# Column sums moved into the last product tile, and a new order of work at the joints

## What is computed

```
def rms_norm(x, w):
    x32 = x.astype(jnp.float32)
    y = x32 * lax.rsqrt(jnp.mean(x32 * x32, axis=-1, keepdims=True) + EPS)
    return (y * w.astype(jnp.float32)).astype(x.dtype)
...
        h = rms_norm(x, mix_norm_pre[l]) * (1.0 + sc_m[:, None, :]) + sh_m[:, None, :]
        y = hybrid_mixer(h, positions, w_in[l], ...)
        x = x + g_m[:, None, :] * rms_norm(y, mix_norm_post[l])
        h = rms_norm(x, ffn_norm_pre[l]) * (1.0 + sc_f[:, None, :]) + sh_f[:, None, :]
        y = swiglu(h, w_gate_up[l], w_down[l])
        x = x + g_f[:, None, :] * rms_norm(y, ffn_norm_post[l])
```

## Time and profile before

| | us |
|---|---|
| median of 3 runs | 3138.99 |
| lowest, highest run | 3138.62, 3145.86 |
| span of the profiled execution | 3139.0 |
| TensorE busy in it | 3038.9 (97%) |
| VectorE busy | 1677.1 (53%) |
| GpSimd busy | 1394.7 (44%) |
| ScalarE busy | 1235.8 (39%) |

### The profile page before, as it was taken

How to read it: one execution, slowest core, us unless ns; L and a number is a source line. 1 busy time by engine, 2 the same in 40 slices (tenths; PEclk the granted TensorE clock), 3 DMA queues, 4 the chain that set the end, 5 groups by cost and what they waited for, 6 DMA issues and landing times.

```text
span 3139.0 us, 40030 instructions
## 1 busy us (share of the span) xinstructions
PE 3038.9 (97%) x14910; PEld 2422.7 (77%) x14910; DVE 1677.1 (53%) x2917; ACT 1235.8 (39%) x2444; POOL 1394.7 (44%) x1196
## 2 busy tenths in 40 slices
PE   6999899999999999999999999999999999999998
PEld 5677778888776788888867687888887677888886
DVE  7787656623677553223385746554245656565521
ACT  3345432233345432233354534434334545343432
POOL 2331255545432254445542545444464335454443
PEclk9998899998999899999999999999999999999999
DMA  5422346632421122322331122232232211223222
GB/s 219 126 86 100 122 169 245 243 105 77 125 81 41 41 84 95 100 93 89 119 101 41 54 81 81 94 101 96 96 110 90 81 48 61 94 81 101 94 93 75
DMA packets 92977, 316.54 MB, mean 101 GB/s; under 512 B 12016, under 2 KB 12656, under 8 KB 92656
## 3 DMA queue, kind: packets, MB, share of 16 engines
q1 hardware_dynamic: 92784, 313.99, 30.1%
HBM read 301.36 MB, written 2.10 MB: 97 GB/s over the span
## 4 chain that ended last, share of the span: by engine, by line
PE 91%; DVE 5%; ACT 1%; issue 1%; DMA 1%; POOL 0%; SPq 0%; DVEq 0%; ACTq 0%
PE bank L199 24%; PE bank L200 23%; PE bank L201 23%; PE bank L1831 2%; PE bank L1852 2%; PE bank L1885 2%; PE bank L418 1%; PE bank L419 1%; DVE sel L1351 1%; PE bank L422 1%; PE bank L534 1%; PE bank L1118 1%; PE bank L958 1%; DVE small L1350 1%; PE bank L432 1%
## 5 line engine op out<-in xcount | busy, mean ns | idle before, releaser
L182 POOL TENSOR_TENSOR wl<-raw,wh 128x512 fp32r<-128x512 f32 (+1 forms) x952 | 1241.0, 1308 | 1571.8 <-ACT wh L171 1571.1
L171 ACT ACTIVATE wh<-raw 128x512 fp32r<-128x512 f32 (+1 forms) x952 | 587.7, 623 | 1369.9 <-PE bank L201 1273.2
L199 PE MATMUL bank<-hh,wh 128*128 128x512 f32 x2368 | 945.6, 399 | 0.8 <-DVE hl L1516 0.4
L200 PE MATMUL bank<-hl,wh 128*128 128x512 f32 x2368 | 925.2, 391 | 0.0
L201 PE MATMUL bank<-hh,wl 128*128 128x512 f32 x2368 | 924.9, 391 | 0.0
L199 PEld LDWEIGHTS bank<-hh,wh 128*128 128x128 f32 x2368 | 446.0, 188 | 128.7 <-issue 34.6
L201 PEld LDWEIGHTS bank<-hh,wl 128*128 128x128 f32 x2368 | 446.0, 188 | 95.5
L200 PEld LDWEIGHTS bank<-hl,wh 128*128 128x128 f32 x2368 | 446.3, 188 | 89.2 <-issue 0.5
L201 PE MATMUL bank<-hidh,wl 128*128 128x512 f32 x704 | 273.9, 389 | 0.0
L199 PE MATMUL bank<-hidh,wh 128*128 128x512 f32 x704 | 273.9, 389 | 0.0
L200 PE MATMUL bank<-hidl,wh 128*128 128x512 f32 x704 | 273.9, 389 | 0.0
(11 more groups left out here) (395 smaller groups left out, 4159.9 us busy)
## 6 DMA issues: line engine op xcount, KB each, us to landing
raw<-in_w SPq DMA_DIRECT2D x444, 512.0 KB, 3.4
mod_raw2a<-in_wmod SPq DMA_DIRECT2D x28, 512.0 KB, 4.6
mod_raw2b<-in_wmod SPq DMA_DIRECT2D x28, 512.0 KB, 4.8
mod_raw<-in_wmod SPq DMA_DIRECT2D x24, 512.0 KB, 4.2
raw<-in_w SPq DMA_DIRECT2D x32, 384.0 KB, 3.0
first_mods<-in_wmod SPq DMA_DIRECT2D x16, 512.0 KB, 13.8
tmp<-rawb SPq DMA_DIRECT2D x72, 64.0 KB, 2.4
turn<-sine SPq DMA_DIRECT2D x56, 64.0 KB, 2.0
```

Source lines behind the costliest of these rows:

```text
L171: act.activation(self.m.wh[:, t % 2, w_], self.m.raw[:, t % RING, w_], ACT.Copy)\
L182: pool.tensor_tensor(self.m.wl[:, t % 2, w_], self.m.raw[:, t % RING, w_], self.m.wh[:, t % 2, w_].bitcast(F32), ALU.subtract)\
L199: pe.matmul(out, wh, xh, start=start, stop=False)
L200: pe.matmul(out, wh, xl, start=False, stop=False)
```

## The change

The sums over acc, gain_sum and cross_sum (24 passes) leave the junction; TensorE does them in the last weight tile of the product, ahead of its last chunk (`first_columns`). In the last junction it is the 8 passes over acc. The sums over the last cross product go ahead of the first spread instead of behind it. That cross product is now made by VectorE from the bank, with the gain, without waiting for y (L401 of the new file), and ScalarE makes y's last tile behind the first root (`last_output`). VectorE does the mean ahead of its first multiply, the second reciprocal right behind it, then adds tile 0, multiplies tiles 1, 2 and 4 by acc (no longer by bank 5), and tile 5 between the first scales. GpSimd waits for the copied inverse alone and multiplies tiles 3, 6 and 7. Two scales and two rests now alternate.

```
+        def first_columns(pe):
+            pe.wait_ge(cross_used if carry else square_used, KD - 1)
+            for tb in range(NT):
+                column(pe, ps[4][:, 2 * tb:2 * tb + 1], m.acc, tb, ones[:, 0:1], start=(tb == 0))
+            if carry:
+                for tb in range(NT):
+                    column(pe, ps[4][:, 2 * tb + 1:2 * tb + 2], gain_sum, tb, ones[:, 0:1])
+                for tb in range(NT):
+                    column(pe, ps[1][:, tb:tb + 1], cross_sum, tb, ones[:, 0:1], start=(tb == 0))
...
                     if c == 3:
                         last.then_inc(s.slot_done[0], 1)
+                    if t == n - 1 and c == s.width(t) // P - 2:
+                        first_columns(pe)
...
+        def last_output(act):
+            act.wait_ge(cross_ready, KD)
+            act.activation(m.y[:, KD - 1, :], ps[banks[(KD - 1) % 2]][:], ACT.Identity, scale=gain[:, KD - 1:KD])\
+               .then_inc(y_ready, 1)
...
+                if carry and last:
+                    dve.wait_ge(square_ready, KD)
+                    dve.scalar_tensor_tensor(m.sq[:, 0, :], ps[banks[nb % 2]][:], gain[:, nb:nb + 1], m.x[:, nb, :],
+                                             ALU.mult, ALU.mult).then_inc(cross_ready, 1)
...
-        OWN = 5
+        OWN = [0, 1, 2, 4, 5]
+        SHARED = [3, 6, 7]
...
-            pool.wait_ge(x_ready, 1)
             pool.wait_ge(inv_copied, 1)
-            pool.wait_ge(col_ready, 2)
+            multiply(3)
+            pool.wait_ge(x_ready, 1)
             update(1)
             update(2)
-            multiply(5)
             update(3)
             multiply(6)
             update(4)
             update(5)
+            update(6)
             multiply(7)
-            update(6)
             update(7)
...
             if pre:
+                last_output(act)
+                act.wait_ge(mean_ready, 1)
+                act.activation(xroot4, mean4, ACT.Sqrt, bias=m.eps[:, 0:1], scale=1.0 / D).then_inc(root_ready, 1)
                 act.wait_ge(added_ready, 1)
                 act.activation(m.acc[:], ps[5][:], ACT.Copy).then_inc(inv_copied, 1)
-                act.wait_ge(mean_ready, 1)
...
-                dve.tensor_tensor(m.y[:, k, :], m.y[:, k, :], ps[5][:], ALU.mult).then_inc(added_ready, 1)
+                inv = m.acc if k else ps[5]
+                dve.tensor_tensor(m.y[:, k, :], m.y[:, k, :], inv[:], ALU.mult).then_inc(added_ready, 1)
```

More of the change, by code:

```diff
@@ L286, in swap_halves, with column @@
             sp.dma_start(dst[at + 32:at + 64], src[at:at + 32]).then_inc(sem, 16)
+    def column(pe, dst, src, tb, w, start=False, stop=False):
+        return pe.matmul(dst, src[:, tb * P:(tb + 1) * P], w, start=start, stop=stop)
     OUT_SEMS = ("square_ready", "square_used", "y_ready", "cross_ready", "cross_used", "weights_set")
@@ L360, in scalar @@
                         act.activation(square(nb), ps[banks[nb % 2]][:], ACT.Square).then_inc(square_ready, 1)
-                    act.activation(m.y[:, nb, :], ps[banks[nb % 2]][:], ACT.Identity, scale=gain[:, nb:nb + 1])\
-                       .then_inc(y_ready, 1)
+                    if nb < KD - 1 or not carry:
+                        act.activation(m.y[:, nb, :], ps[banks[nb % 2]][:], ACT.Identity, scale=gain[:, nb:nb + 1])\
+                           .then_inc(y_ready, 1)
                     if nb < KD - 1:
@@ L381, in vector @@
                         dve.wait_ge(cross_used, nb)
-                    dst = m.sq[:, 0, :] if last else ps[0][:]
-                    dve.tensor_tensor(dst, m.x[:, nb, :], m.y[:, nb, :], ALU.mult).then_inc(cross_ready, 1)
+                    dve.tensor_tensor(ps[0][:], m.x[:, nb, :], m.y[:, nb, :], ALU.mult).then_inc(cross_ready, 1)
                 if last:
@@ L405, in vector @@
                     ins.then_inc(cross_used, 1)
-        return Stage(sync, gpsimd, tensor, scalar, vector)
+        stage = Stage(sync, gpsimd, tensor, scalar, vector)
+        stage.last_output = last_output
+        return stage
     START_SEMS = ("square_ready", "square_used", "xroot_ready", "xdiag_ready", "xinv_ready", "scaled_ready",
@@ L489, in build, with junction @@
               "scaled_ready", "h_head_ready", "h_ready", "order")
[L491 removed]
+    def junction(sems, product, pre, last_output, cols=None):
         (sum_ready, root_ready, col_ready, inv_ready, inv_copied, mean_ready, added_ready, multiplied, x_ready,
@@ L544, in tensor @@
             for tb in range(NT):
-                ins = column(ps[4][:, 2 * tb:2 * tb + (2 if pre else 1)], m.sq[:, 1, :], tb, w_, stop=(tb == NT - 1))
+                ins = column(pe, ps[4][:, 2 * tb:2 * tb + (2 if pre else 1)], m.sq[:, 1, :], tb, w_, stop=(tb == NT - 1))
             ins.then_inc(sum_ready, 1)
             if pre:
+                pe.wait_ge(cross_ready, KD)
                 for tb in range(NT):
-                    column(ps[1][:, tb:tb + 1], cross_sum, tb, ones[:, 0:1], start=(tb == 0))
+                    ins = column(pe, ps[1][:, tb:tb + 1], m.sq[:, 0, :], tb, ones[:, 0:1], stop=(tb == NT - 1))
+                ins.then_inc(sum_ready, 1)
             pe.wait_ge(col_ready, 1)
@@ L552, in tensor @@
             if pre:
[L553 to L556, removed]
                 pe.wait_ge(col_ready, 2)
@@ L617, in vector @@
             dve.tensor_scalar(mean4, mean4, 0.0, None, ALU.max).then_inc(mean_ready, 1)
+            dve.wait_ge(inv_ready, 1)
+            add(0)
+            dve.wait_ge(root_ready, 2)
+            dve.reciprocal(xinv4, xroot4).then_inc(col_ready, 1)
+            dve.wait_ge(added_ready, 1)
+            dve.tensor_tensor(m.x[:, 0, :], m.x[:, 0, :], m.y[:, 0, :], ALU.add).then_inc(x_ready, 1)
             dve.wait_ge(inv_copied, 1)
             add(1)
[L620 to L623, removed]
+            add(2)
+            add(4)
             dve.wait_ge(inv_ready, 2)
@@ L626, in vector @@
             scale(1)
[L627 to L630, removed]
+            rest(0)
+            add(5)
+            scale(2)
+            rest(1)
+            rest(2)
+            scale(3)
+            scale(4)
+            rest(3)
+            rest(4)
+            scale(5)
+            scale(6)
+            rest(5)
+            rest(6)
+            scale(7)
+            rest(7)
         stage = Stage(None, gpsimd if pre else None, tensor, scalar, vector)
```

25 lines of the change are left out of this document (10 added, 15 removed).

## The result

The changed kernel takes 3172.3 us (median of 6 runs, 3166.2 to 3175.6), the kernel before 3138.8 (6 runs, 3132.6 to 3154.5). The ratio is 1.010, 95 % interval 1.0076 to 1.0124: it is slower. The profiled execution has a span of 3164.5 us; it is the shortest of the six (3166.2 us). Of all runs in this document one stands apart, in a slower state: one of fold_fill's nine took 4582 us at a granted clock of 0.61, and its ratio leaves it out.

The account below looks back on a forecast made before the run. TensorE, busy 3038.9 of 3139.0 us, plus its waits bounds the kernel. Per joint 8.8 + 7.1 + 13.3 = 29.2 against 24.86, +4.3 for seven joints, plus 0.85 at the end: 31 us, giving 3170 us, range 3150 to 3180.

Parts of the forecast that it names:

- part 1: Last tile: 24 moved sum passes get no cover, so the product ends 2.6 us later, losing 0.85 us of cover.
- rival (d): Last tile: moved passes slide between product matmuls at no cost; 2.3 us a joint faster, 3123 us; chance 6 %.
- part 2: Joint, from mark (old start of first sum pass) to VectorE's first multiply: 8.8 us against mean 5.26, loss 3.5.
- Rival (b): Joint's sums: clock holds through them, first multiply after 7.3 us, 10 us less in all, 3160 us; chance 10 %.
- part 3: Joint, second spread: reciprocal right behind first multiply, second inverse there after 2.95 us instead of 4.94; 2.0 us won.
- rival (a): Multiplies before first scale: turns cost less, first multiply to matmul 4.9 us, 2.2 less a joint, 3155 us; chance 12 %.
- part 4: First multiply to next stage: VectorE's multiplies take turns with GpSimd over SBUF; 7.1 us against mean 6.45, loss 0.65.
- part 5: Next stage's first matmul to first ordinary one: TensorE stays the bound by 0.9 us; 13.3 us against mean 13.1.
- The last joint: Very end of the kernel: 8 moved passes, formerly covered by the square, cost 0.85 us.
- Spare time of cross_used: Wait of first_columns for cross_used: costs nothing, with 0.1 us to spare in the out product.

Follow-up runs that it names:

- fold_fill: Changed kernel with sums behind the product, bank-5 multiplies, last cross product added into cross_sum by VectorE, and throwaway matmuls in TensorE's waits; 3129.6 us, ratio 0.9972.
- only_cols: Kernel before, with only the sums over acc, gain sum and cross sum moved ahead of the last chunk; 3163.5 us, ratio 1.0081.
- bank_reads: Changed kernel, with VectorE's multiplies reading the inverse from bank 5 again instead of acc; 3154.4 us, ratio 1.0044.
- pool_held: Changed kernel, still reading acc, with GpSimd's first multiply held until VectorE has done its first four; one run, 3163.8 us.
- fill_before: Kernel before, with throwaway 512-column matmuls in each of seven joints, three ahead of the second spread and three behind it; 3140.6 us, ratio 1.0000.
- cols_back: Changed kernel, with the sum passes behind the product's last chunk again; 3154.2 us, ratio 1.005.
- fill_both: Changed kernel with sums behind the last chunk, bank-5 multiplies, and throwaway matmuls, two ahead of the second spread and three behind; 3138.0 us, ratio 0.9996.
- both_back: Changed kernel with sums behind the last chunk again and multiplies reading bank 5 again; 3139.7 us, ratio 0.9999.

## Why the prediction was right

The forecast was 3170 us in a range of 3150 to 3180, and 3172.3 was measured. Term by term:

- **Passes in the tile are paid in full** (part 1): held, 2.57 us on the chain for 2.6. The rival (d) of free passes falls by only_cols.
- **Mark to first multiply** (part 2): 9.17 us for 8.8. The term was short by 0.4 in this profile: in five of seven joints the clock had fallen ahead of the last square's sums, and half of the 0.4 is the slower last chunk (last square's sums at 3.86 for 3.65), the other half these sums. I had taken them between fast and slow, and they were nearly all slow. The two other profiles with the same work have 9.09 and 8.75, so the miss is no larger than the scatter. Rival (b), 7.3 us, falls: the shortest joint has 8.15, and the last chunk doesn't hold the clock.
- **The second spread** (part 3): it starts 0.83 us behind the first multiply, as reckoned. Where nothing else is late it wins 1.86 of its 2 us, as bank_reads shows (4.63 from first multiply to next stage, for the 4.9 of rival (a) and 6.49 before).
- **Turns of VectorE and GpSimd** (part 4): held, and shown by bank_reads and pool_held. First multiply to next stage 6.77 us for 7.1. The detail that was off is the order of the turns: I gave GpSimd the first one, but VectorE's second multiply was 0.04 us ahead of it. The price of the turns, 2.14 us a joint, is near the 2.2 that I had reckoned, and rival (a), no turns, falls. The Trainium skill's GPSIMD Engine Reference, section 8 (Key points), names such contention without a price; the runs agree with it and give the price.
- **Behind the start** (part 5): 13.14 for 13.3, and TensorE didn't wait for low parts. The spare time below that is less than I put: with low parts 0.9 us ahead of their need the stretch could shrink to 12.4, and in fill_before, where the clock is back in time, it takes 12.75.
- **The last joint**: 2.1 us for 0.85. The cover was sized rightly, 0.9; the other 1.2 is the low clock in its sums and spread. That part is scatter of the clock: bank_reads moves the same passes and reaches the first product 4.62 us behind the mark, 0.9 later than before, with its spread at the high clock; fill_before moves none and takes 4.60, with its spread at the low one.
- **Spare time of cross_used**: reckoned as nothing, with 0.1 us to spare, and nothing it was. The profile has a wait of 0.7 us in the four out joints together, but on the weight load of the first pass; the pass itself starts 0.23 us behind the last product matmul, as in the down joints.

The sum of 31 us against 31.7 read in the profile and 33.5 between the medians owes something to errors that cancel, which is luck: 0.4 too little on the first term, 0.5 too much on the next two, and 1.2 too little at the last joint. The share of each part was also misjudged in one way: cols_back and bank_reads each bring back 18 us, where I expected 11 and 12. For the sums, 15 of the 18 us are read in the joints, and what I left out is that the tile's last chunk and what stands behind it slow down too. For bank_reads it is 14 of 18 (29.09 to 27.06, times seven). What is left lies within the intervals of the ratios.

What stays open: whether the change moves the fall of the clock at all. The two profiles have it 1.1 us apart (4.04 and 2.92 behind the old mark), and the thin passes begin 0.7 us earlier; but in the kernel before alone the fall runs from 2.25 to 5.06, and two other profiles with the same work have it the other way round, 3.20 for the work of before and 3.62 for that of the change.

## What to carry to other kernels

Thin work that stands behind a dense stretch may be running in the shadow of a wait; before moving it ahead, measure that shadow, since in the dense stretch here every pass was paid. Remove thin passes rather than move them: folding 8 of 40 into an idle VectorE won 8 us, and moving 24 cost 18 (cols_back) to 23 (only_cols). Read more than one profile before you explain a few tenths of a microsecond that hang on the clock. And when an operand moves from a bank to SBUF, look for who else uses SBUF then: two engines that overlapped may take turns.

## What the runs showed of the hardware

- VectorE and GpSimd took turns where VectorE had two SBUF inputs, and whoever asked first went first, VectorE with a lead of 0.04 us. It costs both sides: a multiply of 0.69 us became 1.75, GpSimd's 1.27 became 1.77. With one operand in a bank both keep their pace (1.88 us for three beside a GpSimd at 1.27).
- TensorE's clock went from 2.4 to 1.2 GHz during the thin sums or right behind them in all seven joints of both kernels, and in the changed one also where three wide matmuls stood between them. Throwaway matmuls of 512 columns in the waits brought it back to 2.4 GHz earlier: six of them 4.7 us (fill_before, 11.5 against 16.2 us behind the mark), five 7.3 us (fill_both, 9.4 against both_back's 16.6).
